# Expert gates of two prompt tiles by indirect additions in memory instead of one-hot matmuls

## The reference

```python
v1, i1 = lax.top_k(s1, 16)          # best 16 of 128 keys, first half of the query
v2, i2 = lax.top_k(s2, 16)          # and of the second half
cand = v1[..., :, None] + v2[..., None, :]
sc, sel = lax.top_k(cand, 16)       # best 16 of the 256 sums
eidx = take(i1 * 128 + i2, sel)     # expert numbers
g = softmax(sc)
act = gelu(einsum('phkd,pd->phk', u[eidx], h))
out = einsum('phkd,phk->pd', v[eidx], g * act)
```

## Time and profile before

| | us |
|---|---|
| median of 3 runs | 3282.55 (3282.47 to 3286.2) |
| the profiled execution | 3285.27 |
| its span, first to last instruction | 3283.5 |
| PE busy | 3231.9 |
| DVE busy | 2310.8 |
| ACT busy | 1100.5 |
| POOL busy | 839.8 |

### The profile page before, as it was taken

How to read it: one execution, slowest core, us unless ns; L and a number is a source line. 1 busy time by engine, 2 the same in 40 slices (tenths; PEclk the granted TensorE clock), 3 DMA queues, 4 the chain that set the end, 5 groups by cost and what they waited for, 6 DMA issues and landing times.

```text
span 3283.5 us, 58975 instructions
## 1 busy us (share of the span) xinstructions
PE 3231.9 (98%) x25438; PEld 2404.9 (73%) x25438; DVE 2310.8 (70%) x3603; ACT 1100.5 (34%) x1154; POOL 839.8 (26%) x544
## 2 busy tenths in 40 slices
PE   8999999999999999999999999999999999999998
PEld 5578888888888655555678888888888885555555
DVE  5979763565655588998955795654656447989887
ACT  4153332342434333333332433233333333333332
POOL 0000000000000477888500000000000006788882
PEclk9999999999999999999999999999999999999999
DMA  9932344363646999899722323444645489998993
GB/s 372 401 123 78 122 166 157 127 224 147 221 158 214 355 350 358 328 372 363 264 91 90 118 78 139 163 158 156 206 160 196 170 283 352 340 359 337 371 370 115
DMA packets 271532, 751.25 MB, mean 229 GB/s; under 512 B 57808, under 2 KB 203360, under 8 KB 236256
## 3 DMA queue, kind: packets, MB, share of 16 engines
q1 hardware_dynamic: 220848, 613.35, 50.6%
q0 software_dynamic: 45088, 134.39, 10.7%
q10 hardware_dynamic: 5392, 0.56, 0.1%
HBM read 615.51 MB, written 132.71 MB: 228 GB/s over the span
## 4 chain that ended last, share of the span: by engine, by line
PE 94%; DVE 3%; DMA 1%; ACT 1%; issue 0%; SPq 0%; DVEq 0%; ACTq 0%
PE PS L848 43%; PE PS L887 33%; PE PS L687 5%; PE PS L877 3%; PE PS L805 3%; PE PS L675 2%; PE PS L778 2%; PE PS L737 1%; DMA ring<-whole_w 1%; ACT ring L1094 1%; PE PS L717 0%; DVE ring L1539 0%; PE PS L818 0%; PE PS L763 0%; DVE H L1515 0%; DMA arena<-whole_w 0%
## 5 line engine op out<-in xcount | busy, mean ns | idle before, releaser
L848 PE MATMUL PS<-X,ring 128*128 128x256 f16 (+1 forms) x12288 | 1434.1, 279 | 2.4 <-ACT arena L1290 2.4
L848 PEld LDWEIGHTS PS<-X,ring 128*128 128x128 f16 x12288 | 1199.6, 98 | 221.7 <-issue 2.9
L887 PE MATMUL PS<-arena,ring 128*128 128x416 f16 (+2 forms) x6336 | 1086.4, 335 | 10.7 <-DVE arena L2015 10.7
L1539 DVE SCALAR_TENSOR_TENSOR ring<-ring 128x4096 f16<-128x4096 f32 x148 | 655.2, 4427 | 604.7 <-ACT ring L1094 604.6
L887 PEld LDWEIGHTS PS<-arena,ring 128*128 128x128 f16 x6336 | 616.1, 98 | 481.1 <-issue 16.7
L1094 ACT ACTIVATE ring<-ring 128x4096 f16<-128x4096 f32 x148 | 535.0, 3615 | 736.4 <-PE PS L887 699.7
L1443 POOL DMA_INDIRECT ACC<-V,arena x128 | 177.1, 1384 | 2169.0 <-DMA gates_dram<-ACC 2111.4
L1448 POOL DMA_INDIRECT arena<-act_dram,arena x256 | 486.0, 1898 | 150.0 <-issue 77.4
L1318 ACT ACTIVATE H<-PS 128x544 f32<-128x544 f32 x256 | 159.9, 625 | 983.6 <-PE PS L848 983.6
L2007 DVE TENSOR_TENSOR arena<-arena 128x416 f32<-128x416 f32 x256 | 218.8, 918 | 124.8 <-PE PS L887 78.0
L1443 POOL DMA_INDIRECT H<-V,arena x128 | 172.4, 1347 | 61.1 <-issue 33.2
(11 more groups left out here) (209 smaller groups left out, 1969.3 us busy)
## 6 DMA issues: line engine op xcount, KB each, us to landing
ring<-U SPq DMA_DIRECT2D x64, 2048.0 KB, 10.4
ring<-V SPq DMA_DIRECT2D x64, 2048.0 KB, 8.3
act_dram<-H SPq DMA_DIRECT2D x64, 1088.0 KB, 5.0
gates_dram<-ACC SPq DMA_DIRECT2D x52, 1024.0 KB, 5.4
arena<-gates_dram SPq DMA_DIRECT2D x32, 1664.0 KB, 16.3
arena<-act_dram SPq DMA_DIRECT2D x64, 768.0 KB, 9.6
ring<-split_w SPq DMA_DIRECT2D x17, 2048.0 KB, 8.3
arena<-whole_w SPq DMA_DIRECT2D x11, 2048.0 KB, 11.7
```

The source lines that it names most:

```text
L848: mm = pe.matmul(ps_row(u)[:, COLS[half]], parts[lane][:, pu, k * 512 + j * P:k * 512 + (j + 1) * P], h16(k, half, ph), start=(k == n == 0 ...
L887: mm = pe.matmul(ps_expert(c, a, b), parts[lane][:, pv, j * D + c * P:j * D + (c + 1) * P], WT[:, grp, pw, j, a:b], start=(first and j == ...
L1539: dve.scalar_tensor_tensor(out=parts[lane][:, 1, :], in0=raw[lane], scalar=scale, in1=parts[lane][:, 0, :], op0=ALU.mult, op1=ALU.subtract ...
```

## The change

Tiles 0 and 1 get their gates in another way. GpSimd writes zeros to their part of the table (64 DMAs per layer of 128 partitions x 4 experts x 128 tokens). VectorE computes, for each token and pick, the place in the table and the gate (`gates_to_add`), and GpSimd issues one indirect DMA per tile and pick that adds 128 floats in memory, 256 per layer. Within a tile the 16 additions of a head wait until those of the head before have landed. Tile 2 (`BUILT`) and the samples keep the one-hot matmuls: 10 batches per layer instead of 26. The order of the tiles is now 0, 1, 2, samples, 3, with 2, 3, 7, 4 and 14 groups.

The table is now [partition, expert of 128, token], so the write of a batch has pieces of 16 tokens, 64 B; a load of gates fetches one group, and `weigh` reads rows. SyncE waits for all additions too before the first loads of gates, and in the V groups a load of gates follows each load of activations.

```diff
+ADDED = (0, 1)
+BUILT = 2
+ROUTE = ADDED + (BUILT, SAMPLE, OWN_TILE)
+SPAN = {0: 2, 1: 3, BUILT: 7, SAMPLE: 4, OWN_TILE: 14}
+ADD_ORDER = tuple((0, h) for h in range(4)) + tuple((t, h + 4 * (1 - t)) for h in range(4) for t in (1, 0)) + \
+    tuple((1, h) for h in range(4, HEADS))
...
-        stage = ACCF[:, 0:4096].rearrange("p (s g t e) -> p s g t e", s=2, g=BODIES, t=BATCH)
+        stage = ACCF[:, 0:4096].rearrange("p (s i t) -> p s i t", s=2, i=NKEYS)
...
-                    sp.dma_start(gates_dram[:, :, dense_at(tile, b):dense_at(tile, b) + BATCH, :],
-                                 stage[:, n % 2, :, :, :]).then_inc(g_written[n % 2], 16)
+                    sp.dma_start(gates.rearrange("p (i t) -> p i t", t=DENSE)[:, :, at:at + BATCH],
+                                 stage[:, n % 2, :, :]).then_inc(g_written[n % 2], 16)
...
+                        for t in ADDED:
+                            sp.wait_ge(gate_added[t], 16 * PICKS * (l + 1))
...
+                if l == 0:
+                    pool.wait_ge(rows_done, 2 * ADA_SLOTS)
+                else:
+                    for lane in range(2):
+                        pool.wait_ge(g_in[lane], 16 * BODIES)
+                for m in range(GROUPS):
+                    for t in ADDED:
+                        pool.dma_start(gate_rows[:, 4 * m:4 * m + 4, t * P:(t + 1) * P],
+                                       zeros[:, :].unsqueeze(1).to_broadcast([P, 4, ZEROS])).then_inc(zeroed, 16)
+                pool.wait_ge(zeroed, 16 * GROUPS * len(ADDED) * (l + 1))
+                for t, h in ADD_ORDER:
+                    if h:
+                        pool.wait_ge(gate_added[t], 16 * TOPK * (HEADS * l + h))
+                    else:
+                        pool.wait_ge(adds_found, len(ADDED) * l + t + 1)
+                    for i in range(TOPK * h, TOPK * (h + 1)):
+                        pool.indirect_dma_start(by_element, bass.IndirectOffsetOnAxis(ap=ADD_I[t][:, i:i + 1], axis=0),
+                                                ADD_W[t][:, i:i + 1], None, compute_op=ALU.add).then_inc(gate_added[t], 16)
...
+                def gates_to_add(tile):
+
+                    link(dve.tensor_scalar(PART_A, KEYS[:, 0, :], float(DENSE), WHICH, ALU.mult, ALU.add))
+                    link(dve.tensor_scalar(PART_A, PART_A, float((tile - OWN_TILE) * P), None, ALU.add))
+                    link(dve.scalar_tensor_tensor(out=PART_A, in0=KEYS[:, 1, :], scalar=float(BODIES * T * 8), in1=PART_A,
+                                                  op0=ALU.mult, op1=ALU.add))
+                    link(dve.tensor_copy(ADD_I[tile], PART_A))
+                    dve.tensor_scalar(ADD_W[tile], GG[:, :, :].rearrange("p h k -> p (h k)"), W_SCALE, None, ALU.mult).then_inc(
+                        adds_found, 1)
...
-                        if i == (0 if tile == SAMPLE else 1):
-                            places(index, n)
+                        if i == (0 if tile in (0, SAMPLE) else 1):
+                            places(index, n)
...
+                            if tile in ADDED:
+                                dve.wait_ge(keys_found, l * len(ROUTE) + TURN_NO[tile])
+                                dve.wait_ge(gates_ready, l * len(ROUTE) + TURN_NO[tile])
+                                gates_to_add(tile)
...
-                    gates = GB[:, (group // 2 % 2) * DENSE * 8:(group // 2 % 2 + 1) * DENSE * 8].rearrange("p (t e) -> p t e", e=8)
                     for j in range(4):
                         a = AB[:, grp, j, :]
-                        dve.tensor_tensor(a, a, gates[:, :, 4 * grp + j], ALU.mult).then_inc(wf_ready, 1)
+                        dve.tensor_tensor(a, a, GB[:, grp, j, :], ALU.mult).then_inc(wf_ready, 1)
```

More of the change, by code:

```diff
@@ L63 @@
 OWN_TILE = 3
-ROUTE = (SAMPLE, OWN_TILE, 0, 1, 2)
-SPAN = {SAMPLE: 4, OWN_TILE: 5, 0: 7, 1: 7, 2: 7}
+ADDED = (0, 1)
[4 more added lines that the diff above has]
+    tuple((1, h) for h in range(4, HEADS))
+ZEROS = 128
 OWN = 128
@@ L72 @@
 V_HOMES = 8
-TILE_BATCHES = {t: (NS_ if t == SAMPLE else P - OWN if t == OWN_TILE else P) // BATCH for t in ROUTE}
+TILE_BATCHES = {t: {SAMPLE: NS_, BUILT: P}.get(t, 0) // BATCH for t in ROUTE}
 NBATCH = sum(TILE_BATCHES.values())
@@ L157, in turn_group @@
         return None
-    return SPAN[tile] - (3 if TILE_BATCHES[tile] == P // BATCH else 2)
+    return SPAN[tile] - (3 if tile == BUILT else 2) if TILE_BATCHES[tile] else None
 def gate_steps(tile, i, j):
[L163 to L173, removed]
+    if tile == BUILT:
+        first = i - (SPAN[tile] - 2)
+        return range(8 * first + 2 * j, 8 * first + 2 * j + 2) if first >= 0 else range(0)
+    return range(j, j + 1) if TILE_BATCHES[tile] and i == SPAN[tile] - 1 else range(0)
 def _u_phase():
@@ L402, in build @@
         KEYS = small[:, 656:912].rearrange("p (j n) -> p j n", j=2)
-        stage = ACCF[:, 0:4096].rearrange("p (s g t e) -> p s g t e", s=2, g=BODIES, t=BATCH)
+        stage = ACCF[:, 0:4096].rearrange("p (s i t) -> p s i t", s=2, i=NKEYS)
+        ADD_W = [part(6784 + 256 * t, P) for t in ADDED]
+        ADD_I = [part(6912 + 256 * t, P, dt=U32) for t in ADDED]
+        zeros = sb("zeros", [P, ZEROS])
         HM = [a.bitcast(F16).rearrange("p (s k t) -> p s k t", s=2, k=KD) for a in (ACCF[:, :], part(8768, KD * T))]
@@ L416, in build @@
         AB = part(0, 2, 4, DENSE)
-        GB = arena[:, 4096:4096 + 2 * DENSE * 8]
+        GB = part(4096, 2, 4, DENSE)
         WT = part(12288, 2 * 4 * DENSE).bitcast(F16).rearrange("p (g s j t) -> p g s j t", g=2, s=2, j=4)
@@ L457, in build @@
         taps_made = sem("taps_made")
-        g_in, w_ready = sem("g_in"), sem("w_ready")
+        g_in, w_ready = [sem(f"g_in{i}") for i in range(2)], sem("w_ready")
+        zeroed, adds_found = sem("zeroed"), sem("adds_found")
+        gate_added = [sem(f"gate_added{t}") for t in ADDED]
         dve_step, pool_step, y_ready, y_out, state_out = (sem(x) for x in "dve_step pool_step y_ready y_out state_out".split())
@@ L508, in _ @@
             sp.dma_start(X[:, :, :], xT).then_inc(x_in, 16)
-            view = gates_dram.rearrange("p g t e -> g p (t e)")
+            gates = gates_dram.rearrange("p g t e -> p (g t e)")[:, 0:NKEYS * DENSE]
+            by_group = gates.rearrange("p (m n) -> p m n", m=GROUPS)
             of_token = act_dram.rearrange("p m (j t) -> p m j t", j=4)
@@ L580, in spill @@
                     n = FIRST_BATCH[tile] + b
+                    at = (OWN_AT if tile == SAMPLE else tile * P) + b * BATCH
                     sp.wait_ge(act_read, U_ACT[l] + GATE_AT[tile, 2 * b + 1] + 1)
-                    sp.dma_start(gates_dram[:, :, dense_at(tile, b):dense_at(tile, b) + BATCH, :],
-                                 stage[:, n % 2, :, :, :]).then_inc(g_written[n % 2], 16)
+                    sp.dma_start(gates.rearrange("p (i t) -> p i t", t=DENSE)[:, :, at:at + BATCH],
+                                 stage[:, n % 2, :, :]).then_inc(g_written[n % 2], 16)
                 m = 0
@@ L611, in _ @@
                 sp.dma_start(X[:, :, :].rearrange("p k t -> p (k t)"), x_dram).then_inc(x_back, 16)
[L613 to L622, removed]
                 def v_turn(body):
@@ L632, in v_turn @@
                                  of_token[:, bass.ds(group, 1), :, :].rearrange("p o j t -> p (o j) t"))
+                        sp.dma_start(GB[:, lane, :, :].rearrange("p j t -> p (j t)"), by_group[:, group, :] if isinstance(
+                            group, int) else by_group[:, bass.ds(group, 1), :].rearrange("p o n -> p (o n)")).then_inc(g_in[lane], 16)
                 with sp.Fori(0, BODIES - 2) as body:
                     v_turn(body)
-                    next_g(body)
                 v_turn(BODIES - 2)
@@ L1339, in take_gates @@
                     u = next_use()
-                    act.copy(stage[:, n % 2, :, SUB * half:SUB * (half + 1), :],
-                             ps(u, 1024).rearrange("p (t g e) -> p g t e", t=SUB, e=8)).then_inc(act_read, 1)
+                    act.copy(stage[:, n % 2, :, SUB * half:SUB * (half + 1)],
+                             ps(u, 1024).rearrange("p (t i) -> p i t", t=SUB)).then_inc(act_read, 1)
                 m = 0
@@ L1350, in _ @@
                                 take_picks()
-                            if (i, j) == ((1, 0) if tile == SAMPLE else (2, 1)):
+                            if (i, j) == {SAMPLE: (1, 0), 0: (1, 1)}.get(tile, (2, 1)):
                                 act.wait_ge(shifted, l * len(ROUTE) + TURN_NO[tile])
@@ L1426, in _ @@
             link(ins)
+            link(pool.memset(zeros[:, :], 0.0))
+            by_element = gates_dram.rearrange("p g t (e o) -> (p g t e) o", o=1)
+            gate_rows = gates_dram.rearrange("p g t e -> p (g t e)")[:, 0:NKEYS * DENSE].rearrange("p (i t) -> p i t", t=DENSE)
             pool.memset(EA[:, :, 0:EA_PAD], 0.0).then_inc(consts_made, 1)
@@ L1949, in hot @@
                     buf = n % 2
```

(20 more changed lines are left out.)

6 lines of the change are left out of this document (2 added, 4 removed).

## The result

The changed kernel takes 3332.53 us (median of 4 runs, 3330.84 to 3332.81) where the kernel before takes 3282.78 (3282.47 to 3286.2): a ratio of 1.0145, interval 1.0132 to 1.0157. It is 49.8 us slower. The forecast was 3267.

What follows compares the result with a forecast made beforehand. TensorE, busy for 98% of the span, was taken as the bound. -58.6 + 7.6 + 37 = -14 us, with one more for the turns, gave 3267 us from a median of 3282.55; range 3226 to 3430.

Steps and rivals of the forecast that it cites:

- slow drain: Rival, slower: memory drains the short gate writes slowly, 3778 us at s = 54, 3405 at s = 23; chance 0.26.
- s: Time one batch's write of gates in 64 B pieces needs on the DMA engines, taken as 11.6 us.
- Matmuls: TensorE, U groups: tiles 0 and 1 lose 32 batches of gate matmuls at 1.83 us, -58.6 us.
- VectorE at the start: Start of U groups: tile 0's candidates and places delay group 2's low half, 3.8 us a layer, +7.6.
- Additions: GpSimd's 256 indirect DMAs per layer, taken at 1.5 us each, end at 836 us and stay hidden: 0.
- Late additions: Rival, slower: additions at 2.8 us each end some 120 us after SyncE needs them, 3470 us; chance 0.08.
- Zeroing: GpSimd's 64 zero writes per layer beside the weight loads: counted 0, with 0 to 15 us in the range.
- The gates' write: Tile 2's batch writes in 64 B pieces outlast the 7.39 us between batches and queue, stalling TensorE: +37 us.
- 6s - 51: Formula for TensorE's stall per layer, waiting for a PSUM buffer behind the queued writes: 18.6 us.
- Gates' loads: V groups: same bytes in loads half as long, VectorE reads rows, TensorE doesn't wait for them: 0.
- The write is hidden: Rival, faster: s under 8.5, so the write causes no stall; -51 us, 3231 us; chance 0.14.

Runs made afterwards that it cites:

- e6_all: The changed kernel with tile 2's batches one per group, layer 0's zeros after the residual's store, and three groups for tile 0: 3225.47 us, ratio 0.9817 to the kernel before.
- e1_wide: The changed kernel with the gates' write in longer pieces, same bytes (512 B for tile 2, 128 B for samples): 3248.51 us, ratio 0.9883 to the kernel before.
- e5_spread: The changed kernel with tile 2's eight batches one per group instead of four, 64 B pieces kept: 3249.14 us, ratio 0.9890 to the kernel before.

## Why the prediction was wrong

The time lies within the stated 3226 to 3430, but that is luck: the upper part was there for a slow drain with s up to 25, and there was none. The forecast was faster, and the kernel is slower. Term by term:

- *Matmuls, -58.6:* right. 640 gate matmuls are left, and "e6_all" is 58.7 us faster than before.
- *VectorE at the start, +7.6:* right. TensorE wants group 2 at 352.3 + 44.5 = 396.8. VectorE's timeline has the low half behind candidates and places:

```profile
396.45 4.42 DVE L1554 SCALAR_TENSOR_TENSOR ring<-ring 128x4096 f16<-128x4096 f32 x1
```

 and TensorE's timeline the wait, 3.99 us where 3.8 was forecast (8.9 in two layers came back with a third group):

```profile
400.93 3.25 PE L842 MATMUL PS<-X,ring 128*128 128x256 f16 x14 [3.99 <-DVE ring L1554]
```

- *Additions, 0:* hidden, as said, but not at the pace that was taken. The line's view:

```profile
L1447 POOL DMA_INDIRECT gates_dram<-arena x512: 1532/1542/5773, 417.9 to 2649.6; - x171
```

 One takes 1.54 us in the median, up to 5.77, and 1.92 in the mean (984.9 us of busy time over 512); with 0.3 between them the cycle is 2.2 us, the upper bound of the prediction. Its lower bound came from a wrong line: the 0.94 us in the earlier trace rows is a gather of rows of v (L1443), and a gather of single floats (L1448) took longer there, also where no low half met it:

```profile
1194.49 1.37 POOL L1448 DMA_INDIRECT arena<-act_dram,arena  x1 [0.30 <-issue]
```

 (L1448's least in the whole run is 0.94 too, its median 1.36.) They run to 1016 us, not to under 900, and the V groups follow the U groups without a wait for them. "Late additions" did not happen. Their 14.6 us beside the queue of writes were not in the sum.
- *Zeroing, 0:* wrong, 12 to 15 us, the top of its bounds. The prediction looked at the weight loads with their slack; what was late was a store that VectorE waits for, which had no slack of that size. GpSimd's part was near the cheap end: the last zeros are issued at 254.
- *The gates' write, +37:* this is the step that failed. It costs 84 us (changed kernel less "e1_wide"), 42 a layer where 18.6 stood; the additions' 14.6 lie within that. The stall "6s - 51" was the right kind. s was too small, 12.9 us and not 11.6, which by the same formula makes 26.4 a layer, 7.8 more. Measured are 30.4 us of idle time and 11.6 of slower matmuls. About 22 of the idle time are the stall itself, TensorE waiting for ScalarE's copies (44.7 in two layers), so the formula is 4 too high there. Another 8 are waits for the U slot (23.2 less the start's 7.2 in "e1_wide", in two layers): the formula had its load only as traffic between two writes, not as something that TensorE waits for. SyncE issues it late; whether an earlier issue would have helped, with the writes' pieces in the same queue, no run tells. The 11.6 us are matmuls at the lower clock, 0.90 over the 174 us in either layer, where "e1_wide" has 1.00. A pause of TensorE was priced at its length; here it cost its length and a good third more.
 That s came so near is luck. The prediction took the time of the packets as the price of a piece. In the changed kernel q1's packets take 148.1% of 16 engines (the row of 610 to 640 us above), so they overlap in time; read in the same way one takes 18.7 ns of an engine, and a batch would need 19.2 us. The pace of the pieces, 1.27 per ns, is what gives 12.9.
- *Gates' loads, 0:* right, by the V groups' unchanged length.
- *The slow drain:* didn't happen. A lone write lands after 15.0 us ("e5_spread"), not over 20: some 12 to 13 of drain and the rest around it, where s = 23 would make 25. *The write is hidden* is what happens once the batches are spread or the pieces doubled.

By its own steps with their measured sizes the sum is -58.6 + 8.9 + 12.1 + 84 = +46 by differences of medians, and with differences of the ratios (10.5, 14.1, 86.0) it is +52; measured +49.8.

## What to carry to other kernels

When a table's layout changes, count the pieces of its writes as well as the bytes, and compare the drain with the time between two writes: here 12.9 against 7.39 us lost 84, and the same writes, one every 24 us, lost nothing that shows. Then ask what stands behind such a write in its issuer's list, since the issue itself took up to 17.5 us here while earlier pieces were waiting, and 0.4 where none were. Price a short piece by how many pass in a stretch of time, not by the time of one packet. Filler work without a near deadline, like these zeros, is started behind the stores that somebody waits for.

## What the runs showed of the hardware

- An issue can hold SyncE, and not by its number of pieces alone: 16384 pieces kept it 7.3 us in the median and 17.5 at most in the changed kernel, where the writes queue, and 0.38 in the median in "e5_spread", where they don't. The activations' store behind such writes took SyncE 13.2 us, behind a single one 6.8 to 7.5, and 0.34 with no such write ahead of it.
- Packets of 64 B overlap in time: their times add up to 148.1% of 16 engines.
- Pieces of 64 and of 128 B cost the same each, 0.74 ns over all engines, and pieces of 512 B 1.9, start and end of the write included.
- While the writes queued, the granted clock was 0.90 over 174 us with 30.4 us of pauses, and the matmuls took 11.6 us longer than the same work at 1.00 in "e1_wide".
- An indirect DMA that adds takes GpSimd 1.53 us at the least and 1.54 in the median for 128 floats; the gathers of 128 floats in the kernel before took 0.94 at the least and 1.36 in the median.
- 16 MB of zeros from GpSimd took a store of SyncE's from 5.7 to 19.8 us, and loads of 2 MB from 8.9 to 24.9.
